# Issuing the reloads of turned attention rows from GpSimd instead of ScalarE, and loading past keys and values earlier

## What is computed

```python
h = rms_norm(x, norm_g)                       # x: 512 prompt rows, or 8 sampled rows, of 2048
u, gp, q, k, v, ga = split_proj(h, w_in)      # one 2048 x 6144 projection, six parts of 1024
pm = pool_mix(u, history, pos0, pool_w, pool_scale)     # trailing means over 2/4/8/16, then 256x256
a = dilated_attn(q, k, v, past_k, past_v)     # 16 heads of 64; windows (128,1), (512,4), (2048,16)
mix = concat([pm * silu(gp), a * silu(ga)])
y = rms_norm(x + mix @ w_out, final_g)        # w_out: 2048 x 2048
```

## Time and profile before

| | |
|---|---|
| Median of 3 runs | 821.46 us (821.45 to 824.18) |
| The profiled execution | 821.09 us, of which the span from the first to the last instruction is 819.3 us |
| PE busy | 807.1 us (99%) |
| DVE busy | 627.4 us (77%) |
| ACT busy | 398.9 us (49%) |
| POOL busy | 203.2 us (25%) |
| Transfers | 150.04 MB, mean 183 GB/s |
| Granted TensorE clock | 0.996 of full |

### The profile page before, as it was taken

How to read it: one execution, slowest core, us unless ns; L and a number is a source line. 1 busy time by engine, 2 the same in 40 slices (tenths; PEclk the granted TensorE clock), 3 DMA queues, 4 the chain that set the end, 5 groups by cost and what they waited for, 6 DMA issues and landing times.

```text
span 819.3 us, 17483 instructions
## 1 busy us (share of the span) xinstructions
PE 807.1 (99%) x6625; PEld 802.6 (98%) x6625; DVE 627.4 (77%) x1347; ACT 398.9 (49%) x875; POOL 203.2 (25%) x340
## 2 busy tenths in 40 slices
PE   9999999999999999999999999999999999999995
PEld 8999999999999999999999999999999999999994
DVE  4657895897589778958885897689888886777765
ACT  4745435533554454345435533553465345555554
POOL 2103502520360045014402610450000131222220
PEclk9999999999999999999999999999999999999998
DMA  8569647856774696578558756884668567766565
GB/s 297 142 173 232 168 125 171 231 144 168 188 208 122 163 233 169 152 175 228 152 141 186 204 147 182 193 214 123 172 195 272 156 181 203 207 184 174 150 180 218
DMA packets 271499, 150.04 MB, mean 183 GB/s; under 512 B 44448, under 2 KB 261472, under 8 KB 271392
## 3 DMA queue, kind: packets, MB, share of 16 engines
q1 hardware_dynamic: 239784, 118.97, 53.7%
q0 software_dynamic: 12672, 20.59, 9.9%
q10 hardware_dynamic: 18960, 9.38, 4.0%
HBM read 119.49 MB, written 28.27 MB: 180 GB/s over the span
## 4 chain that ended last, share of the span: by engine, by line
PE 87%; DVE 6%; DMA 3%; issue 1%; ACT 1%; SPq 1%; POOL 1%; DVEq 0%; ACTq 0%
PE pj L889 64%; PE pj L1048 13%; PE ps_s L946 1%; PE ps_s L948 1%; PE ps_o L977 1%; PE ps_o L975 1%; DMA out<-arena 1%; PE ps_o L889 1%; DVE w_lo L1624 1%; PE ps_t L995 1%; PE ps_s L995 1%; PE ps_s L889 1%; PE ps_s L827 1%; DVE arena L1755 1%; DMA w_raw<-in_w_out 0%
## 5 line engine op out<-in xcount | busy, mean ns | idle before, releaser
L889 PE MATMUL pj<-mov_hi,w_hi 128*128 128x260 f32 (+1 forms) x1632 | 332.1, 285 | 0.3 <-DVE mov_lo L1645 0.3
L889 PE MATMUL pj<-mov_hi,w_lo 128*128 128x260 f32 (+1 forms) x1632 | 328.3, 283 | 0.0
L889 PE MATMUL pj<-mov_lo,w_hi 128*128 128x260 f32 (+1 forms) x1632 | 327.8, 282 | 0.0
L889 PEld LDWEIGHTS pj<-mov_hi,w_hi 128*128 128x128 f32 x1632 | 252.7, 189 | 2.1 <-issue 0.6
L889 PEld LDWEIGHTS pj<-mov_lo,w_hi 128*128 128x128 f32 x1632 | 251.4, 188 | 0.0
L889 PEld LDWEIGHTS pj<-mov_hi,w_lo 128*128 128x128 f32 x1632 | 251.4, 188 | 0.0
L1148 ACT ACTIVATE w_hi<-w_raw 128x640 fp32r<-128x640 f32 (+1 forms) x157 | 121.4, 773 | 228.5 <-PE pj L889 159.3
L1624 DVE TENSOR_TENSOR w_lo<-w_raw,w_hi 128x640 fp32r<-128x640 f32 (+1 forms) x157 | 135.5, 863 | 62.7 <-ACT w_hi L1148 62.3
L1566 POOL DMA_DIRECT2D p_scratch<-extra x168 | 104.8, 631 | 82.4 <-DVE extra L1727 79.9
L1597 POOL DMA_DIRECT2D y_scratch<-arena x56 | 37.6, 678 | 110.5 <-DVE arena L2209 81.3
L1540 POOL DMA_DIRECT2D out<-arena x8 | 4.6, 569 | 213.0 <-DMA arena<-arena 213.0
(11 more groups left out here) (275 smaller groups left out, 1295.3 us busy)
## 6 DMA issues: line engine op xcount, KB each, us to landing
w_raw<-in_w_in SPq DMA_DIRECT2D x96, 320.0 KB, 4.1
w_raw<-in_w_in SPq DMA_DIRECT2D x48, 384.0 KB, 4.5
arena<-in_cache_k_win SPq DMA_DIRECT2D x16, 384.0 KB
arena<-in_cache_v_win SPq DMA_DIRECT2D x16, 384.0 KB
p_scratch<-extra POOLq DMA_DIRECT2D x112, 48.0 KB, 3.3
w_raw<-in_w_out SPq DMA_DIRECT2D x26, 192.0 KB, 3.0
arena<-in_cache_k_win SPq DMA_DIRECT2D x8, 512.0 KB
arena<-in_cache_v_win SPq DMA_DIRECT2D x8, 512.0 KB
```

The lines of the kernel that those rows point to most:

```text
L889: mm = pe.matmul(dst[h][:, 0:own.stop - own.start], w, m[:, k, own], start=(k == 0 and i == 0), stop=(c == 2 and k == KT - 1 and i == 2))
```

## The change

Three things, and the renaming of counters that goes with them. First, `load_turned` moves from ACT's program to POOL's: 8 transfers a pair in pairs 0 to 6, 56 in all, each with its waits. Second, POOL's list is reordered around them: the key row (`send_k_row`) is sent after units 0 and 1 of head 0 instead of before unit 0. Third, SP loads the keys at j = 4, 5, 6 instead of 5, 6, 7 and the values at j = 7, 8, 9 instead of 10, 11, 12. The counters `y_in` of the output stage are now shared with three of `mov_in`, which have reached 32 by then, and the reloads have counters of their own (`p_in`).

```diff
--- before.py
+++ after.py
@@ -104,7 +104,7 @@
 TURN_SLOT = (0, 1, 0)
 TURN_AT = (0, 384)
 OUT_ST = (Y_ST * 4 * SENT, Y_ST * 2 * SENT, 0)
-OUT_IN = tuple(16 * len(u) * 2 * SENT for u in UNITS)
+OUT_IN = (32, 32, 32)
 
 
 C_ID, C_DIST, C_NLOG, C_SLOPE, C_SB, C_INV, C_IW, C_OWN, C_END = np.cumsum(
@@ -426,7 +426,8 @@
         mix_back = [sem(f"mix_back{i}") for i in range(len(RELOADED))]
         m_hi_done, m_split = sem("m_hi_done"), sem("m_split")
         yt_done = sem("yt_done")
-        y_st, y_in = [sem(f"y_st{i}") for i in range(3)], [sem(f"y_in{i}") for i in range(3)]
+        y_st, p_in = [sem(f"y_st{i}") for i in range(3)], [sem(f"p_in{i}") for i in range(3)]
+        y_in = [mov_in[i] for i in (8, 9, 10)]
         y_added, y_squared = sem("y_added"), sem("y_squared")
         xr_in = [sem(f"xr_in{i}") for i in range(3)]
         y_scaled = sem("y_scaled")
@@ -735,10 +736,10 @@
                         if pr % 2 == 1:
                             sp.dma_start(pw_raw, pw[pr // 2:pr // 2 + 1].rearrange(
                                 "a p c d -> (a p) c d")).then_inc(pw_in, 16)
-                    if j in (5, 6, 7):
-                        load_keys(pr, j - 5)
-                    if j in (10, 11, 12):
-                        load_values(pr, j - 10)
+                    if j in (4, 5, 6):
+                        load_keys(pr, j - 4)
+                    if j in (7, 8, 9):
+                        load_values(pr, j - 7)
                     if j in (6, 8, 12):
                         spread_rows(pr, (6, 8, 12).index(j))
                     if j == 14:
@@ -1210,19 +1211,8 @@
                                            "p (j x) -> p j x", j=i + 1), ACT.Copy)
                 a.then_inc(pt_hi_done, 1)
 
-            def load_turned(pr, h, u):
-
-                act.wait_ge(y_st[TURN_SLOT[u]], Y_ST * (turns_sent(pr, h, u) + 1))
-                if 2 * pr + h > 0:
-                    act.wait_ge(pv_done, 2 * pr + h)
-                for i, at in UNITS[u]:
-                    n = P * (i + 1)
-                    act.dma_start(pt_lo[:, 0:i + 1, P * i:P * i + P].bitcast(F32),
-                                 p_dram[6 * pr + 3 * h + u, at:at + n].rearrange(
-                                     "(j p) q -> p j q", p=P)).then_inc(y_in[u], 16)
-
             def p_hi_sent(pr, h, u):
-                act.wait_ge(y_in[u], 16 * len(UNITS[u]) * (2 * pr + h + 1))
+                act.wait_ge(p_in[u], 16 * len(UNITS[u]) * (2 * pr + h + 1))
                 if u == 0 and 2 * pr + h > 0:
                     act.wait_ge(pv_done, 2 * pr + h)
                 for i, at in UNITS[u]:
@@ -1244,9 +1234,6 @@
                     p_hi(pr, 0, j - s0 - 3)
                 if p is FINAL and s1 + 3 <= j < s1 + 6:
                     p_hi(pr, 1, j - s1 - 3)
-                for h in range(2):
-                    if p is not FINAL and p.s[h] + 5 <= j < p.s[h] + 8:
-                        load_turned(pr, h, j - p.s[h] - 5)
                 if s0 + 2 <= j < s0 + 5:
                     norm_unit(pr, 0, j - s0 - 2)
                 if s1 + 2 <= j < s1 + 5:
@@ -1566,6 +1553,17 @@
                     pool.dma_start(rows[:, :, own], turn_slot(u)[own, :].rearrange(
                         "p (b r) -> p b r", r=SQ)).then_inc(y_st[TURN_SLOT[u]], 16)
 
+            def load_turned(pr, h, u):
+
+                pool.wait_ge(y_st[TURN_SLOT[u]], Y_ST * (turns_sent(pr, h, u) + 1))
+                if 2 * pr + h > 0:
+                    pool.wait_ge(pv_done, 2 * pr + h)
+                for i, at in UNITS[u]:
+                    n = P * (i + 1)
+                    pool.dma_start(pt_lo[:, 0:i + 1, P * i:P * i + P].bitcast(F32),
+                                 p_dram[6 * pr + 3 * h + u, at:at + n].rearrange(
+                                     "(j p) q -> p j q", p=P)).then_inc(p_in[u], 16)
+
             for pr in range(PAIRS):
                 if pr > 0:
                     g = pr // 2 - 1
@@ -1576,17 +1574,26 @@
                                 continue
                             pool.wait_ge(pool_mixed, 2 * g + dt + 1)
                             pool.dma_start(mix_dram[2 * g + dt], z_gp[dt]).then_inc(pmix_st, 16)
-                send_k_row(pr)
                 if pr < SENT:
-                    for u in range(3):
-                        send_turned(pr, 0, u)
+                    send_turned(pr, 0, 0)
+                    send_turned(pr, 0, 1)
+                    send_k_row(pr)
+                    load_turned(pr, 0, 0)
+                    send_turned(pr, 0, 2)
+                else:
+                    send_k_row(pr)
                 if pr > 0:
                     send_split(pr - 1 + PAIRS)
+                if pr < SENT:
+                    load_turned(pr, 0, 1)
+                    load_turned(pr, 0, 2)
                 send_v_row(pr)
                 send_u(pr)
                 if pr < SENT:
                     for u in range(3):
                         send_turned(pr, 1, u)
+                    for u in range(3):
+                        load_turned(pr, 1, u)
 
 
             def send_tile(d):
```

## The result

The changed kernel takes 834.66 us (median of 832.34 to 835.36), the kernel before 822.76 us on the same chip: a ratio of 1.0119, 95% interval 1.0085 to 1.0152. The ratios in this text are those on record with their intervals and not plain quotients of two medians; for this pair of medians the quotient is 1.0145. The forecast was 822.7 us in a range of 820.7 to 825.5. The profiled execution took 832.34 us with a span of 830.2 us, 10.9 us more than the span before.

A forecast was written before the change was run, and what follows sets the result against it. PE was taken as the bound, busy for 807.1 of 819.3 us. Terms 0 + 0 + 0 + 1.5 us gave 822.6 on the profiled 821.09 and 823.0 on the runs' median; forecast 822.7 us, range 820.7 to 825.5.

The forecast's parts named there:

- In the usual pairs neither is waited for by PE or needed before j = 17: Loading keys and values sooner, outside the last pair: PE doesn't wait for either; cost and gain 0.
- Bytes move away: Earlier key and value loads in the usual pairs take bytes from the steps where the stores run; cost and gain 0.
- 2.7 us: Pair 6, chunk 8: weight split ends 2.7 us before PE needs it, the smallest such cover found from the second pair on.
- L1733: VectorE's last subtraction before PE's product with head 1's values; cover 0.67 us in pair 0, 2.0 in 5, 0.17 in 6.
- Pair 7: Last pair: spread key row behind more loads, GpSimd's key row 2.0 us later, landing 1.5 us later; cost 1.5 us.
- Removal from ScalarE: Taking reloads off ScalarE removes waits and issues, but PE never waits for that weight split; worth 0 in time.
- Adding to GpSimd: 56 reload issues of 0.62 us on GpSimd; head 1's unit 0 in at 557.1 us, 1.4 us to spare; cost 0.
- late reloads: Rival: head 1's reloads need over 4.8 us, so PE's product with the values waits; 5.3 us, 826.4 us; chance 8%.
- held issues: Rival: each GpSimd issue waits for a VectorE instruction to end; 0.9 us, 822.0 us, or 823.5 with last pair's; chance 3%.
- I am wrong if PE waits inside the usual pairs: Sign against the forecast, which expected PE busy for all of 28 to 600 us again.

The follow-up runs named there:

- e4: Changed kernel with the values back at steps 10, 11, 12, keys still early and reloads on GpSimd; 823.11 us, ratio 0.9986 to the kernel before.
- e6: Changed kernel with the values of pair 0 alone back at steps 10, 11, 12; 828.43 us, ratio 1.0038 to the kernel before.
- e1: Kernel before with only SyncE's earlier key and value steps, reloads staying on ScalarE; 834.56 us, ratio 1.0115.
- e2: Changed kernel with SyncE's old load steps, so only GpSimd's reloads and new list order remain; 826.33 us, ratio 1.0010 to the kernel before.
- e11: Kernel before with keys at 4, 5, 6 and values at 9, 10, 11, reloads still on ScalarE; 821.77 us, ratio 0.9966.
- e3: Changed kernel with SyncE's old load steps in pairs 0 and 7 alone; 827.09 us, ratio 1.0030 to the kernel before.
- e10: Changed kernel with keys back at steps 5, 6, 7 and values still at 7, 8, 9; 858.09 us, ratio 1.0399 to the kernel before.
- e13: Changed kernel with the spread rows issued ahead of the key or value tile of the same step; 846.92 us, ratio 1.0271 to the kernel before.
- e5: Changed kernel with the values issued by ScalarE at its steps 6, 7, 8 instead of by SyncE; 834.17 us, ratio 1.0113 to the kernel before.
- e14: Changed kernel with each value tile split in two transfers of four batches, the second at steps 10, 11, 12; 853.57 us, ratio 1.0366.
- e15 to e17: Long runs replacing 512-byte pieces: changed kernel's values, 826.11 us; the same with keys at 5, 6, 7, 840.15 us; changed kernel's keys and values, 824.05 us.
- e12: Changed kernel with early values in pair 0 alone, the other seven pairs back at steps 10, 11, 12; 828.06 us, ratio 1.0039 to the kernel before.
- e8: Changed kernel with the values one step early, at 9, 10, 11, instead of three; 822.66 us, ratio 0.9959 to the kernel before.

## Why the prediction was wrong

- **What failed** is the step "In the usual pairs neither is waited for by PE or needed before j = 17, and bytes move away from the steps in which the stores run. Cost and gain 0." It asked who needs the values, and not who stands behind them. e4 and e6 show the cost to be the early values', with and without pair 0; e1 shows nearly all of the change's loss with the loads alone. No rival of the prediction had a late weight chunk in it. "Bytes move away" was true of steps 10 to 12 and left out that they move to the weight chunks of steps 8 to 10, the spread query row and the spread key row.
- **The cover was counted for the wrong reader.** 2.7 us is how early PE's weights are split. PE never waited for them after the change either. But the same late split holds up the softmax and the parts behind it in ScalarE's and VectorE's lists, and PE's scores and transpositions depend on these. The parts of head 1 had only 1.7 us of cover in every one of pairs 0 to 6, which the trace of the kernel before shows; the chunk in question came 4.1 us later and the parts 6.0. I had written this kind of cover down for L1733 only, and had counted chunks from pair 1 on; the first loss was in pair 0.
- **The stall's price** had no term for the clock: of the 5.2 us in pair 0, 1.7 were half clock after a wait of 2.45 us.
- **Pair 7**: mechanism right, size off. Key row 4.9 us late, forecast 2.0 (bounds 0.7 and 3.3); landing 5.85 us, forecast 7.4; VectorE's idle time 3.56 us, forecast 2.3; PE's waits 2.47 + 0.49 us, forecast 1.9; cost 2.8 us, forecast 1.5, within the bound of 3.8. The term that was mis-sized is the delay of the key row: I priced the value tile at the stretch's mean rate, whereas the four spread transfers behind it took 5.02 us in issue, 2.87 before, and the history ahead of them 3.18, 1.43 before. By e2's profile a part of this wait may come without the early values.
- **Removal from ScalarE**: 0 forecast, and e2 and e11 measure no effect of it. **Adding to GpSimd**: 0.75 us an issue in the median instead of 0.62, busy 243.9 us (238 forecast), landing 3.9 us in the median instead of 3.4, between 2.0 and 6.4 where the bounds were 2.0 and 6.7. The copy of unit 0 stands at 561.94 - 6.7 = 555.2 us by the old clock (557.1 forecast), after a wait of 0.88 us (2.4 forecast). The rivals of late reloads and held issues did not come: ScalarE waits 1.4 us in all for reloads, and no issue of a reload took more than 775 ns.
- The named sign "I am wrong if PE waits inside the usual pairs" came true: pair 0 runs by the usual plan, and PE waits 0.73 and 2.45 us in it. e3, e10 and e13 have such waits in middle pairs as well.

**What stays open** is which resource is used up. The stretch from 52 to 60 us, before and after:

```profile
52.00:60.00 8.00, 8.00 (x68) 7.92 (x67) 4.73 (x15) 5.01 (x11) 0.61 (x1) 1.00 0.81 193
```
```profile
52.00:60.00 8.00, 8.00 (x67) 7.92 (x67) 2.92 (x9) 1.30 (x3) 0.00 (x0) 1.00 0.66 145
```

The transfer engines are busy for 0.66 of the time at 145 GB/s, less than before, while SyncE is held in its issues; so it isn't their mean rate. Whether some of the engines are full while others idle no view here shows. SyncE's own list (e5), the order within a step (e13) and the early amount (e14) don't explain the loss by themselves; reading in short pieces is the largest part shown (e15 to e17). That two half transfers cost more than a whole one isn't explained.

## What to carry over

When a load is moved earlier, list what is issued right behind it at the new place, and count for each late item the cover of everything that stands behind its consumer in an in-order list, not only that of the consumer. The first and the last round need their own count, since e3, e6 and e12 put most of the loss there. Look at the pieces in which a tile is read, not only at its bytes: the same bytes at the same steps cost 1.2% in pieces of 512 bytes and nothing measurable in long runs.

## What the runs showed of the hardware

- Half clock for 3.40 us followed PE's wait of 2.45 us in pair 0 of the changed kernel, and in e1 those of 2.41 and 2.10 us (it began at 64.9 and 611.0 us). Behind the 2.47 us in pair 7 of the changed kernel, the longest of the four, there was none (1.00 from 608 to 612 us). In e3 it lasted longer, until about 310.2 us, behind a wait of 2.43 us that ended at 303.83.
- A SyncE issue of a small spread transfer (16 KB) took 0.64 us on average for the key row in pair 0 of the kernel before (2.55 us for four), 1.5 us behind a value tile (6.02 for four), and 2.3 us in e5, where ScalarE issued the tiles (9.07 for four).
- The key row's landing fell from a median of 7.4 us to 1.9 us in the changed kernel, with one of 5.85 us left in pair 7. It takes both halves of the change: with the early loads alone (e1) the median is 6.6 us, with GpSimd's new order alone (e2) 4.8.
- With loads one step earlier the runs of the same program agreed within 1.6 us (e8: 822.04 to 823.63), where those of the kernel before are spread over 7 us.
